# Encoder layer on one core: in the branch merge stage the group mean is subtracted plainly, and loads, sums and turns move between units

## The reference, cut to what matters

```python
y = ys[0] + ys[1]
mu = jnp.mean(y, axis=-1, keepdims=True)
var = jnp.mean(jnp.square(y - mu), axis=-1, keepdims=True)
y = ((y - mu) * lax.rsqrt(var + GN_EPS)).reshape(B, S, RWKV_WIDTH) * gn_w + gn_b
bonus = jnp.sum(r_h * k.reshape(hs) * r_k, axis=-1, keepdims=True) * v_h
g = jax.nn.sigmoid(gd) @ gate_up
out = (y + bonus.reshape(B, S, RWKV_WIDTH)) * g
...
merged = g_a * y_a + g_b * y_b
```

## Time and profile before

| | us |
|---|---|
| median of 3 runs | 2604.48 |
| lowest and highest run | 2592.59 and 2606.74 |
| the profiled execution, its own time | 2611.54 |
| its span, from the first to the last instruction | 2609.7 |

### The profile page before, as it was taken

The page is one execution under the profiler, slowest core; times in us unless marked ns, Lnnn a source line. Parts: engine busy times, 40 slices in busy tenths (PEclk is TensorE's granted clock), DMA queues, the critical chain, the costliest instruction groups (busy, mean ns, idle before and its releaser), DMA issues. The chain is left out here.

```text
span 2609.7 us, 53639 instructions
## 1 busy us (share of the span) xinstructions
PE 2378.9 (91%) x22387; PEld 1892.2 (73%) x22387; DVE 1689.9 (65%) x2495; ACT 1106.9 (42%) x1933; POOL 775.1 (30%) x511
## 2 busy tenths in 40 slices
PE   4999999999997999999889799998998996999887
PEld 2778777788886888888878666666876884566664
DVE  5644478966563565656477566766986885666664
ACT  3310134344441555655455455553122221666664
POOL 2122144545442444544123200002300000445443
PEclk7999999999998998999999899999999997999999
DMA  7233434443435133222143611104746445999994
GB/s 306 93 135 136 145 114 138 146 163 121 149 120 175 52 100 91 84 78 77 44 143 105 164 34 31 31 10 163 246 154 227 154 145 222 321 344 335 339 309 98
DMA packets 196193, 394.07 MB, mean 151 GB/s; under 512 B 39856, under 2 KB 105168, under 8 KB 182896
## 3 DMA queue, kind: packets, MB, share of 16 engines
q1 hardware_dynamic: 173776, 322.58, 36.9%
q0 software_dynamic: 12960, 36.59, 5.1%
q10 hardware_dynamic: 9216, 31.46, 3.0%
HBM read 294.57 MB, written 106.48 MB: 154 GB/s over the span
## 5 line engine op out<-in xcount | busy, mean ns | idle before, releaser
L99 PE MATMUL ps_in<-h_t_low,w_in_high 128*128 128x512 f32 x960 | 381.2, 397 | 0.0
L100 PE MATMUL ps_in<-h_t_high,w_in_low 128*128 128x512 f32 x960 | 374.2, 390 | 0.0
L101 PE MATMUL ps_in<-h_t_high,w_in_high 128*128 128x512 f32 x960 | 373.9, 389 | 0.0
L99 PEld LDWEIGHTS ps_in<-h_t_low,w_in_high 128*128 128x128 f32 x960 | 180.2, 188 | 47.6 <-issue 9.3
L1269 POOL TENSOR_TENSOR wkv_levels<-wkv_nt,level_mask 128x1024 f32<-128x1024 f32 x60 | 140.5, 2360 | 238.3 <-ACT wkv_nt L1214 238.3
L101 PEld LDWEIGHTS ps_in<-h_t_high,w_in_high 128*128 128x128 f32 x960 | 180.2, 188 | 38.0
L100 PEld LDWEIGHTS ps_in<-h_t_high,w_in_low 128*128 128x128 f32 x960 | 180.4, 188 | 35.0
L508 ACT COPY p_row<-ps_in 128x512 f32<-128x512 f32 x72 | 42.1, 589 | 288.3 <-PE ps_in L101 244.7
L3092 PE MATMUL ps_xy<-w_tile,hidden_turned 128*128 128x512 f32 x272 | 126.6, 609 | 30.3 <-DMA w_tile<-in_w 28.9
L330 POOL CAST w_in_high<-w_in_tile 128x1024 fp32r<-128x1024 f32 x40 | 47.6, 1190 | 342.4 <-PE ps_in L101 341.0
L2979 POOL TENSOR_TENSOR row_gate<-row_gate,latents_then_v 128x1024 f32<-128x1024 f32 x34 | 81.4, 2394 | 176.0 <-ACT row_gate L3170 170.3
(11 more groups left out here) (434 smaller groups left out, 6314.1 us busy)
## 6 DMA issues: line engine op xcount, KB each, us to landing
merged_t<-in_w SPq DMA_DIRECT2D x36, 1024.0 KB, 16.6
w_tile<-in_w SPq DMA_DIRECT2D x34, 1024.0 KB, 18.4
w_now<-in_w SPq DMA_DIRECT2D x30, 1024.0 KB, 15.8
wkv_in<-front_area SPq DMA_DIRECT2D x24, 1024.0 KB, 5.0
w_in_tile<-in_w_in SPq DMA_DIRECT2D x40, 512.0 KB, 3.6
front_area<-in_w_ada SPq DMA_DIRECT2D x8, 2048.0 KB, 9.4
p_t<-p_mixed ACTq DMA_DIRECT2D x24, 512.0 KB, 3.3
gates<-p_mixed ACTq DMA_DIRECT2D x16, 768.0 KB, 4.0
```

The source lines that it names most:

```text
L99: nc.tensor.matmul(out, w[0], x[1], start=start, stop=False)
L100: nc.tensor.matmul(out, w[1], x[0], start=False, stop=False)
L101: return nc.tensor.matmul(out, w[0], x[0], start=False, stop=stop)
```

## The change

Three things change, all in `finish_and_merge`.

1. `mean` divides the head sum by 64 with an instruction of its own, after a wait for the sum (new semaphore `head_sum`), and `centre` becomes a plain subtraction of two tensors.
2. SP calls `load_rk(j+1)` ahead of the gate load of unit 4j + 2, instead of behind that of unit 4j + 3, and `load_y(j+2)` at 7 instead of 6. PE does the bonus sums at 3 instead of 2, and the transposes and the output gate at 6 instead of 5, now the transposes first. DVE does `bonus` at 5, `affine` at 7 and `gated_out` at 8, each one unit later.
3. Ahead of the units DVE splits the second and third part of the source (`om_low`) before it computes `head_rk`, instead of after.

```diff
@@ sync
             for u in range(len(units)):
+                for j in range(N):
+                    if u == PITCH * j + 2 and j + 1 < N:
+                        load_rk(j + 1)
                 if u + GB < len(units):
                     load_gate(u + GB)
...
                 for j in range(N):
-                    if u == PITCH * j + 3 and j + 1 < N:
-                        load_rk(j + 1)
                     if u == PITCH * j + 5 and j + 1 < N:
                         load_v(j + 1)
-                    if u == PITCH * j + 6 and j + 2 < N:
+                    if u == PITCH * j + 7 and j + 2 < N:
                         load_y(j + 2)
@@ tensor
-                    if u == PITCH * j + 2:
+                    if u == PITCH * j + 3:
                         bonus_sums(j)
-                    if u == PITCH * j + 5:
+                    if u == PITCH * j + 6:
+                        turn(j)
                         output_gate(j)
-                        turn(j)
@@ vector
             def mean(j):
                 dve.wait_ge(m["summed"], j + 1)
-                nc.vector.tensor_reduce(st[:, j % 2, 0], by_head(j % 2), AX.X, ALU.add).then_inc(m["mean"], 1)
+                nc.vector.tensor_reduce(st[:, j % 2, 0], by_head(j % 2), AX.X, ALU.add).then_inc(m["head_sum"], 1)
+                dve.wait_ge(m["head_sum"], j + 1)
+                nc.vector.tensor_scalar(st[:, j % 2, 0], st[:, j % 2, 0], 1.0 / CH, None, ALU.mult).then_inc(m["mean"], 1)

             def centre(j):
                 dve.wait_ge(m["mean"], j + 1)
-                nc.vector.scalar_tensor_tensor(out=by_head(j % 2), in0=spread(st[:, j % 2, 0]), scalar=-1.0 / CH, in1=by_head(j % 2),
-                                               op0=ALU.mult, op1=ALU.add).then_inc(m["centred"], 1)
+                nc.vector.tensor_tensor(by_head(j % 2), by_head(j % 2), spread(st[:, j % 2, 0]), ALU.subtract).then_inc(m["centred"], 1)
...
             w_low(0)
+            om_low(1)
+            om_low(2)
             dve.wait_ge(m["ones_in"], 16)
             for f in range(RF):
                 ins = nc.vector.tensor_scalar(head_rk[:, f], head_ones[:], col(consts, "r_k", f, 1), None, ALU.mult)
             ins.then_inc(m["head_rk"], 1)
-            om_low(1)
-            om_low(2)
...
-                    if at == 4:
+                    if at == 5:
                         bonus(j)
-                    if at == 6:
+                    if at == 7:
                         affine(j)
-                    if at == 7:
+                    if at == 8:
                         gated_out(j)
```

More of the change, by code:

```diff
@@ L2157, in finish_and_merge @@
             "gd_in", "up_in", "ones_in", "tanh", "sig", "head_rk", "om_hi", "om_lo", "oa_hi", "oa_lo", "w_hi", "w_lo", "full", "gated", "added",
-            "rk_in", "v_in", "summed", "rk", "mean", "centred", "squared", "var", "var_in", "sqrt", "inverse", "normed",
+            "rk_in", "v_in", "summed", "rk", "head_sum", "mean", "centred", "squared", "var", "var_in", "sqrt", "inverse", "normed",
             "bonus_full", "gate_full", "turned", "bonus", "affine", "oa")}
```

## The result

The changed kernel takes 2635.43 us (median of 4 runs, 2632.23 to 2637.55); the kernel before took 2605.61 in the runs beside it. The ratio is 1.0127, with a 95% interval of 1.0107 to 1.0148: slower, by 29.8 us between the medians.

The account below looks back on a forecast made before the run. TensorE was taken to set the pace, with VectorE close behind. Terms of 22.9 + 1.1 + 1.5 = +25.5 us on a median of 2604.5 gave 2630 us, range 2608 to 2642.

Parts of the forecast that it names:

- the main term: Four periods, y of rounds 2 to 5, each from T (end of bonus sums): +22.9 us, 86.9 against 64.0.
- the high bound of the queue: On SP's queue, y lands behind everything ahead of it, at T + 10.3; T + 10.2 was taken.
- the lower clock: After its idleness, TensorE runs unit 4j+11 at a lower clock, as unit 1 did: 1.5 us added.
- That y is late because r and k stand ahead of it: In SP's queue, r and k go out from T + 0.2 and y behind them, the last near T + 2.2.
- rival A: Four periods: y not held by r and k, landing T + 7.5; period 18.6, +10.4, time 2617; chance 0.28 with mixtures.
- The wait of the small multiplication: In each period VectorE's small multiplication stands beside POOL until T + 15.2; without the wait, periods 1.2 us shorter.
- The subtraction at nothing: VectorE's centring as a plain subtraction costs nothing, 1.22 us against 1.21; collision with POOL stays possible.
- Ahead of the units: Stage start: TensorE's idleness moves from before unit 1 to before unit 2 (near 5), at lower clock: +1.1 us.
- At unit 24 and behind: Wait for the source's split at unit 24, +0.5; behind it gated_out(4) on a late VectorE, +1; together +1.5 us.
- B: Periods: waiting for y costs about what credited items return; period 16 to 17, 2600 to 2610; chance 0.14.
- C: Faster: TensorE's waits for POOL at bonus sums and part of unit 24's wait go, -3.6; 2600; chance 0.03.
- D: SP's queue: r and k are not loaded sooner; part of the forecast, with no chance of its own.

Follow-up runs that it names:

- e10: The changed kernel with TensorE issuing the output gate's four matmuls three times instead of once in rounds 1 to 4; 2626.39 us, ratio 1.0106.
- e1: The changed kernel with SP's two loads (r and k, y) back where they were before; 2611.42 us, ratio 1.0036.
- e4: The changed kernel with y still at 7, but r and k called right behind it instead of ahead; 2622.29 us, ratio 1.0074.
- e5: The changed kernel with mean and centring as before the change, so no small multiplication; 2636.89 us, ratio 1.0112.
- e3: The kernel before with only the mean and centring changed (small multiplication and plain subtraction); 2606.04 us, ratio 1.0021.
- e7: The changed kernel with the second and third split of the source back behind head_rk; 2635.98 us, ratio 1.0114.
- e9: As e4, with the load of r and k one more unit behind y; 2619.78 us, ratio 1.0062.
- e6: The changed kernel with oa_low(1), the second split of the finished source, one unit later on VectorE; 2633.17 us, ratio 1.0089.
- e8: The kernel before with only the bonus sums at 3 instead of 2 and bonus at 5 instead of 4; 2607.5 us, ratio 1.0001.
- e12: e8 plus oa_high(0) ahead of round 5's square, and VectorE starting with splits, gate_unit(0), then head_rk, fin_gate scaling behind unit 1; 2596.46 us, ratio 0.9973.

## Why the prediction was right

The forecast was 2630 us, slower; 2635.43 came out, inside the range.

**The mechanism, step by step.** With T = 1820.75, the forecast of the main term against the first period:

| step | forecast | measured |
|---|---|---|
| y issued | T + 1.8 | T + 3.2 |
| y landed | T + 10.2 | T + 10.6 |
| directions added | T + 12.6 | T + 12.9 |
| small multiplication done | T + 15.2 | T + 15.3 |
| unit 11 starts, after idleness of | T + 16.0, 5.1 | T + 16.0, 4.9 |
| bonus sums start | T + 20.3 | T + 21.2 |

Up to unit 11 all steps hold to within half a microsecond, save y's issue, which is late because one of the two gate tiles behind r and k took over 1 us to issue. The landing still fits the high bound of the queue. Counted from the issue of r and k, y landed after 10.2, 9.9, 9.4 and 10.1 us, where the bound gives 10.1, and 9.4 for the third period, which has no weight load. So when y's own issue goes out within that burst made no difference that shows. The step that was too small is **the lower clock**: 1.5 us was taken from unit 1, and unit 11 took 5.2 against the 2.84 us of e10 at the full clock, so 2.4. In unit 1 the lower clock ended some 3.3 us after the unit's start, in unit 11 it lasted to the unit's end. (The recorded sum also loses 0.2 us: 16.0 + 3.0 + 1.5 is 20.5, not 20.3.) From their starts to the next bonus sums units 11, 15, 19 and 23 took 5.2, 5.3, 4.4 and 5.3 us, 8.8 together over the full clock, where 6.0 was forecast: 2.8 of the 3.7 us by which the term of 22.9 fell short.

**That y is late because r and k stand ahead of it** is shown, but as 12.1 of the 25.6 us by which e1's four periods are shorter (e4). The other 13.5 come with y's own later place. The prediction has the same split in its two sums, though it does not say so: rival A, with y not held back but called as late, was +10.4 for the four periods, and the forecast +22.9, so 12.5 for what stands ahead of y. The first of these two was too small, the second right.

**The wait of the small multiplication** was the right choice: 1.04 us in the four periods and 2.31 us in round 1, always until POOL is done. e5 prices it at 5.0 us of the stage, 4.3 of them in the four periods, though more than half of that lies in one of them. The Trainium skill (SBUF — State Buffer, Who interferes with whom) has the rule for it; now there is a row at 16 elements that agrees.

**The subtraction at nothing**: in the change no centring is held any more (1.21 or 1.22 us in all six rounds; before, five of the six took 2.01 to 3.39), but by the new order, not by the kind of instruction. e3 shows it held once, and POOL held in its place in four rounds, which cost 4.5 us in the four periods of that kernel.

**Ahead of the units**: +1.4 against +1.1, with 5.76 us of idleness ahead of unit 2 for "near 5".

**At unit 24 and behind**: +4.1 together against +1.5. The first half came out better (-1.8 for +0.5: with longer periods the centring had lost its lateness, and TensorE waited 0.97 us). The second, "up to +1.6, I take +1", was the poorest term: +5.9. Of this, 2.9 us are lower clock that the same code did not pay in e4, e7, e9 and e10; there it is +3.0. The term looked at `gated_out(4)`, and not at `gated_out(5)`, which the same shift puts against `oa_low(1)`: e6 takes 2.3 of the 3.0 away by one line. Without the 2.9 us the stage would have been 29.2 us longer, with 25.5 forecast.

**The rivals.** A (y not held up, periods of 18.6) fell: they are 22.5 in the mean. B and C needed y earlier, C within 3.6 us of its issue, and no round of the change showed it under 7.35. D was right in its facts, r and k go out no sooner, and was part of the forecast. Of the rivals A came nearest when the order was mended but the place kept: e4's periods average 19.5, with y landing 7.7 us after T, where A had 7.5.

## What to carry to other kernels

A load that waits for its buffer holds back all that stand behind it in its queue, so the load with the least slack goes first, and moving its neighbour ahead of it cost the transfer of that neighbour here, not the issue alone. Before moving a step that releases a load, follow the release to the load's user, and count the queue between them; then check each later step of the same shift for a new neighbour on a full engine, not just the first. And when an engine with a large share of idleness ahead of short bursts sets the pace, the idleness can be paid twice, once as waiting and once as a lower clock behind it, and the second part need not come in every execution.

## What the runs showed of the hardware that was not expected

- The landing of the same 1 MB of y took 5.3 to 5.9 us with r and k issued 3.5 to 5.1 us behind (before), 6.6 to 7.3 with them 1 us behind (e4), and 7.35 to 8.0 with them 1.5 to 2.9 us ahead (after). Only the last was foreseen. But the order alone does not set it: with r and k 1.9 us or more behind, it took up to 7.75 us in e3, 8.05 in e1 and 8.27 in e8.
- One gate tile's issue behind r and k took 1.45 us at 1821.54 in the kernel after, where others take 0.33, with no wait that the profile shows.
- Added work on TensorE made a stage shorter: e10, with 64 matmuls more in its trace, has a stage 8.8 us shorter than after, 8.3 of them in the four periods.
- The same wait of TensorE, 1.9 us ahead of unit 26, was followed by a granted clock of 0.52 in the kernel after and of 1.00 in e7.
- Two VectorE splits of 2.29 us beside a POOL addition took 6.70 us (e12), and the addition 4.18 instead of 2.37. A small multiplication of 128x16, 0.17 us alone, took 1.04 to 2.31 beside a POOL multiplication (after).
- The same scan took 417 or 428 us in two executions, at 0.97 or 0.95 of the clock. One profiled span is no measure of a change of this size. The stage is a better one, down to about 3 us.
